# A fused transformer block on Trainium2: tokens loaded first, a convolution ahead of level exponents, and the expert loop's scatter after the up projection

## The chip, the core and the metric

One core of a Trainium2 chip runs the whole block as one program. The metric is the device time of that core in microseconds, the median over several executions. All data are float32. Five engines take part: TensorE (PE; its weight loads are PEld), VectorE (DVE), ScalarE (ACT), GpSimd (POOL) and the queue engine SyncE (SP), which here issues every DMA.

## What is computed

One layer over 256 latent and 256 context tokens of width 1024. The reference, cut to the parts that the change touches (`...` marks what is left out):

```python
hl = modulate(rmsnorm(xl, norm1_g[i]), mod_l[0], mod_l[1])      # h = x / rms * g * (1 + scale) + shift
hc = modulate(rmsnorm(xc, norm1_g[i]), mod_c[0], mod_c[1])
fl = mixer_inputs(hl, p, grid_rows)                             # h @ w_in, short convolutions, decays
...
(gla_c, gla_l), (rw_c, rw_l), (ssd_c, ssd_l) = token_mixers(fc, fl)
xl = xl + mod_l[2] * mixer_output(fl, gla_l, rw_l, ssd_l, p)
hl = modulate(rmsnorm(xl, norm2_g[i]), mod_l[3], mod_l[4])
xl = xl + mod_l[5] * moe(hl, p)                                 # then a final rmsnorm

def moe(h, p):                                                  # top 4 of 32 experts
    ...
    for e in range(N_EXPERTS):
        gu = t @ p['moe_w_gu'][e] + p['moe_b_gu'][e]
        glu, lin = jnp.split(gu, 2, axis=-1)
        ...
        act = glu * jax.nn.sigmoid(SWIGLU_ALPHA * glu) * (lin + 1.0)
        y = y + gates[:, e:e + 1] * (act @ p['moe_w_down'][e] + p['moe_b_down'][e])
```

## The kernel before, in words

Every engine has a program of its own, written out in order; semaphores tie them together. PSUM is handled by a table of rounds (`Rounds`, `round_table`): each named product ("B", "l3", "xs0", "roots") has a group of banks, PE *claims* it (waits until the product before it in that group is drained), *fills* it, and DVE or ACT *drain* it. Groups 0 to 3 are pairs of banks, group 4 is one bank. Three stages are touched.

**The opening** (up to the first projection). SP issues the small parameters, the identity matrix, then for each of eight blocks k of 128 features a piece of the modulation weights (`load_ada(k)`, 1 MB) and one called `opened` (block k of the transposed tokens, beside the first projection weights for it). The four `tokens` transfers (512 KB each, tokens by rows) come behind block 0's two. ACT squares and sums the token rows (line 880), takes the root (883), DVE the reciprocal (1320), and PE spreads the 512 reciprocals over all partitions (`roots_spread`, PSUM "roots"). PE also computes the modulation: `modulation_row(k)` needs block k's two transfers, ACT copies the row (875), `modulation_columns(k)` turns it, DVE adds the bias (1309, 1317). DVE multiplies the raw transposed tokens by the spread reciprocals (1322 for k = 0, 1307 later), ACT and DVE write the modulated hidden state hT (889, 1325), and PE multiplies it by the weights of block k and goes on to the modulation of block k + 1. To fill its waits PE runs `stay_busy(n)`, n products of the identity (line 1986), with n from `WARM`. Each float32 matmul stands in the trace as two records.

**The levels.** The gated linear attention is computed over eight nested block sizes. For level i + 1 POOL forms exponent arguments (lines 788 to 791) in one of two buffers, ACT exponentiates (`level_exp(i)`, line 945), DVE multiplies them with the keys (`level_keys(i)`, line 1424), PE multiplies in two parts (`level(i+1, 0)` and `level(i+1, 1)`, rounds "l0" to "l8" of group 2), and DVE writes the scores out with a mask (`level_out(i)`: 1249, 1251 and 1254), which drains that round. Beside them PE computes the projections B, C, xs0, xs1, z0 and z1. B and xs0 share PSUM group 0, so xs0 can start only when DVE has drained B. B's convolution is begun by ACT (`conv_start`, 899), done by DVE in 12 instructions that read PSUM (`convolve`, 1345) and ended by ACT (906). DVE also folds incoming modulation weights into sums (`multiplied(n)`, 1290 and 1292).

**The expert loop.** All 32 experts are computed, each for 64 slots of tokens. Expert n needs six weight blocks of 2048 KB (four of w_gu, two of w_down). They are brought by SP into a ring of eight slots; `load_slot` (668) waits until PE has freed the slot. Three further slots take weights of expert 20 ahead of the loop. PE's order in `expert` is: `up`, eight steps k over the hidden dimension, two steps a ring slot. After step 0 it calls `between`, which is `scatter_before`: the matmuls that add the previous expert's output to the first half of the tokens (`scatter(…, (0,))`, two matmuls, one for each half of the columns), then two transposes that select the tokens of the next scatter (`select_back`, 2860). After up comes the second half's scatter, then `turn` (2869) of the first activated half, the gather of a later expert's tokens, `turn` of the second half, and `down`. DVE reads up's result for the activation (1864 to 1871) and, after down, writes the expert's weighted output `ye` (1893). The matmuls here go through a helper at line 1972, those of scatter being the 64-row ones. The last expert uses `up_by_halves`, which finishes one half of the columns early.

Of the kernel before, what the change touches and what calls it, by code (L numbers as in the profile page):

```python
# [169 lines left out]
WARM = (10, 4, 26, 7)  # L170
# [21 lines left out]
def round_table():  # L192
    t = []
    for m in range(KD):
        t += [(f"row{m}", 4, 1), (f"col{m}", 2, 1 if m == KD - 1 else 0)]
        if m == 0:
            t.append(("roots", 2, 0))
# [77 lines left out]
def hybrid_block(nc, a):  # L275

    with ExitStack() as ctx:
# [202 lines left out]
        ident_in = sem("ident_in")  # L480
# [10 lines left out]
        silu_c, root_ready, rms_ready, mod_ready = named("silu_c root_ready rms_ready mod_ready")  # L491
# [18 lines left out]
        f_sq, out_ready, out_done, half_up, bias_up = named("f_sq out_ready out_done half_up bias_up")  # L510
# [76 lines left out]
        for s, width, kind, n in loads:  # L587
            base[s] += 1
# [41 lines left out]
        def _(sp):  # L630
# [11 lines left out]
            sp.dma_start(Cb(C_ID), a["consts"][:, 0:P]).then_inc(ident_in, 16)  # L642
            for k in range(KD):
                if k == 1:
                    for i in range(4):
                        sp.dma_start(xtok[:, i, :], a["tokens"][i]).then_inc(x_in[i], 16)
                load_ada(k)
                sp.dma_start(opened[:, k, :], a["opened"][k]).then_inc(slot_full[ADA_SLOTS[k]], 16)
                if k in (3, 6):
                    load_ada(8 + k // 4)  # L650
# [204 lines left out]
        def _(act):  # L855
# [16 lines left out]
            def row_copied(m):  # L872

                R.arrived(act, f"row{m}")
                R.drained(f"row{m}", act.copy(modrow[:, 64 * m:64 * m + 64], pair(f"row{m}", 512)[:, 64 * m:64 * m + 64]))

            row_copied(0)
# [6 lines left out]

            for k in range(KD):
                act.wait_ge(mod_ready, k + 1)
                if k == 0:
                    act.wait_ge(rms_ready, 2)
# [63 lines left out]

            level_exp(0)
            level_exp(1)
            conv_start("B")
# [302 lines left out]
        def _(dve):  # L1258
# [18 lines left out]

            def multiplied(n):
# [24 lines left out]
            for k in range(KD):  # L1303
                s, nth = place["opened", k]
                dve.wait_ge(slot_full[s], 16 * nth)
                if k:
                    step(dve.tensor_tensor(raw[:, k, :], raw[:, k, :], pair("roots")[:, 0:NT], ALU.mult))
# [10 lines left out]
                if k == 0:  # L1318
                    dve.wait_ge(root_ready, 1)
                    dve.reciprocal(small[:, 12:16], small[:, 8:12]).then_inc(rms_ready, 1)  # L1320
                    R.arrived(dve, "roots")
# [646 lines left out]
        def _(pe):  # L1968
# [919 lines left out]
            def expert(m, i, gathers, opening=None, aside=None, past=False):  # L2888
# [25 lines left out]
                if not first:  # L2914
                    scatter((i + 1) % 2, (1,))
# [163 lines left out]
```

## Time and profile before

| | us |
|---|---|
| median of 3 runs (1314.92, 1322.54, 1323.43) | 1322.54 |
| the profiled execution, its whole device time | 1317.88 |
| its span, first to last instruction | 1316.1 |

The span of the profiled execution is 1.8 us below its device time; what is taken from the trace is compared with 1317.88, which is 4.7 below the median. PE is busy for 1246.7 us of the span (95%), DVE for 401.6, ACT for 261.2, POOL for 50.4. The DMA engines move 456.13 MB. The granted TensorE clock is 0.996 of full speed on average. Times below are microseconds from the start of the span; a number in square brackets behind an instruction is how long its engine stood idle before it and what ended that.

### The profile page before, as it was taken

What the parts mean: (1) busy time and instruction counts of PE and PEld (TensorE: products, weight loads), DVE (VectorE), ACT (ScalarE), POOL (GpSimd) and SP (SyncE); (2) the same over time, 40 slices, a digit from 0 to 9 for tenths busy, and PEclk for the clock granted to TensorE, in tenths of its full rate; (3) what the DMA queues carried; (4) which work ended last, traced back from release to release, by engine and by line L of the source; (5) the groups of instructions that cost most, each with busy time, mean ns of one, the idle gap of its engine ahead of it and who ended that gap; (6) DMA issues with size and microseconds to landing.
All of it is one profiled execution on the core that took longest, in us unless ns stands there. A gap on an engine that the chain in (4) does not pass through costs nothing.

```text
span 1316.1 us, 22353 instructions
## 1 busy us (share of the span) xinstructions
PE 1246.7 (95%) x9546; PEld 589.9 (45%) x9546; DVE 401.6 (31%) x906; ACT 261.2 (20%) x601; POOL 50.4 (4%) x89
## 2 busy tenths in 40 slices
PE   8999999889899999999999999999999999999997
PEld 6464656678874333333333333333333333333333
DVE  1457766654442211121111221211221111121112
ACT  3142218543332110111100110100111010011001
POOL 0022100311100000000000000000000000000000
PEclk9999999999999999999999999999999999999999
DMA  9953520243479999999999999999999999999994
GB/s 377 397 193 128 220 108 1 90 144 96 125 279 384 425 426 427 428 429 429 426 429 429 430 427 427 429 430 429 427 428 427 428 428 427 428 427 428 426 427 200
DMA packets 41407, 456.13 MB, mean 347 GB/s; under 512 B 4624, under 2 KB 4880, under 8 KB 12912
## 3 DMA queue, kind: packets, MB, share of 16 engines
q1 hardware_dynamic: 41328, 454.96, 83.1%
q8 instruction: 64, 1.05, 0.3%
q14 instruction: 15, 0.12, 0.0%
HBM read 453.89 MB, written 1.05 MB: 346 GB/s over the span
## 4 chain that ended last, share of the span: by engine, by line
PE 84%; DVE 6%; DMA 5%; issue 2%; ACT 1%; POOL 0%; SPq 0%; DVEq 0%
PE PS L1972 80%; DMA arena<-in_moe_w_gu 3%; DMA arena<-in_moe_b_down 2%; PE PS L2869 2%; DVE arena L1865 1%; DVE arena L1868 1%; DVE arena L1871 1%; PE PS L2860 1%; DVE arena L1345 1%; PE PS L1986 1%; DVE arena L1864 1%; DMA arena<-in_opened 1%; PE PS L2464 0%; POOL arena L790 0%; DVE arena L1965 0%
## 5 line engine op out<-in xcount | busy, mean ns | idle before, releaser
L1972 PE MATMUL PS<-arena 128*64 128x512 f32 (+12 forms) x9174 | 1200.3, 402 | 26.0 <-issue 10.4
L1972 PEld LDWEIGHTS PS<-arena 64*64 64x64 f32 (+6 forms) x9174 | 549.4, 144 | 627.4 <-issue 563.6
L1864 DVE TENSOR_SCALAR arena<-PS 128x256 f32<-128x256 f32 x64 | 38.6, 604 | 505.8 <-PE PS L1972 505.8
L1178 ACT ACTIVATE arena<-arena 128x256 f32<-128x256 f32 x64 | 26.7, 417 | 477.2 <-DVE arena L1864 477.2
L1893 DVE TENSOR_TENSOR arena<-PS,arena 128x512 f32<-128x512 f32 x32 | 22.1, 692 | 214.5 <-PE PS L1972 214.5
L1188 ACT COPY arena<-PS 128x256 f32<-128x256 f32 x32 | 11.9, 373 | 281.0 <-PE PS L2860 281.0
L2869 PE MATMUL PS<-arena 128*128 128x128 f32 x128 | 26.3, 287 | 32.6 <-DVE arena L1871 32.6
L1169 ACT ACTIVATE arena<-PS,arena 128x128 f32<-128x128 f32 x128 | 48.2, 457 | 35.7 <-PE PS L1972 35.7
L2869 PEld LDWEIGHTS PS<-arena 128*128 128x128 f32 x128 | 14.3, 141 | 59.9 <-DVE arena L1871 43.0
L1630 DVE COPY arena<-PS 128x384 f32<-128x384 f32 (+2 forms) x48 | 23.4, 490 | 54.1 <-PE PS L1972 53.7
L1865 DVE TENSOR_SCALAR arena<-PS 128x256 f32<-128x256 f32 x64 | 39.1, 612 | 0.0
L1345 DVE SCALAR_TENSOR_TENSOR arena<-PS,arena 128x255 f32<-128x255 f32 (+5 forms) x68 | 32.6, 481 | 20.2 <-ACT arena L980 14.0
L1292 DVE SCALAR_TENSOR_TENSOR arena<-arena 128x2048 f32<-128x2048 f32 x14 | 33.1, 2363 | 7.0 <-DMA arena<-in_ada 6.9
L1091 ACT COPY arena<-PS 128x384 f32<-128x384 f32 (+2 forms) x48 | 20.5, 427 | 58.7 <-PE PS L1972 58.6
L1868 DVE SCALAR_TENSOR_TENSOR arena<-arena 128x256 f32<-128x256 f32 x64 | 27.2, 425 | 3.9
L1871 DVE TENSOR_TENSOR arena<-arena 128x256 f32<-128x256 f32 x64 | 27.2, 426 | 2.3
L1183 ACT COPY arena<-PS 128x256 f32<-128x256 f32 x64 | 23.7, 370 | 4.3 <-PE PS L2869 4.3
L1840 DVE TENSOR_SCALAR arena<-arena 128x128 f32<-128x128 f32 x64 | 19.1, 342 | 0.0
L1986 PE MATMUL PS<-arena 128*128 128x128 f32 x94 | 14.5, 323 | 3.3 <-DMA arena<-in_consts 3.3
L2860 PEld LDWEIGHTS PS<-arena 128*128 128x128 f32 x64 | 6.5, 141 | 24.3 <-issue 24.3
L1827 DVE TENSOR_SCALAR arena<-arena 128x64 f32<-128x64 f32 x64 | 15.7, 308 | 2.0 <-PE PS L1972 1.9
L1986 PEld LDWEIGHTS PS<-arena 128*128 128x128 f32 x94 | 13.7, 233 | 3.5 <-DMA arena<-in_consts 3.3
(263 smaller groups left out, 395.0 us busy)
## 6 DMA issues: line engine op xcount, KB each, us to landing
arena<-in_moe_w_gu SPq DMA_DIRECT2D x124, 2048.0 KB, 22.5
arena<-in_moe_w_down SPq DMA_DIRECT2D x63, 2048.0 KB, 24.3
arena<-in_ada SPq DMA_DIRECT2D x24, 1024.0 KB, 7.4
arena<-in_w_in SPq DMA_DIRECT2D x4, 2048.0 KB, 9.6
arena<-in_moe_w_gu SPq DMA_DIRECT2D x32, 256.0 KB, 3.0
arena<-in_opened SPq DMA_DIRECT2D x8, 576.0 KB, 19.0
arena<-in_tokens SPq DMA_DIRECT2D x4, 512.0 KB, 8.5
arena<-in_w_out SPq DMA_DIRECT2D x2, 1024.0 KB, 5.8
```

The source lines that it names most:

```text
L1169: ins = act.activation(hg[:, buffer, k, :], PS[:, bank, P * j:P * j + P], ACT.Identity, bias=scales[:, 1, k:k + 1], scale=scales[:, 0, k:k ...
L1178: act.activation(sgm[:, 256 * half:256 * half + 256], glu[:, 256 * half:256 * half + 256], ACT.Sigmoid, scale=ALPHA).then_inc(sig_ready, 1)
L1183: act.copy(actT[:, 2 * half:2 * half + 2].rearrange("p a b c -> p (a b c)"), src).then_inc(actT_ready, 1)
L1292: ins = dve.scalar_tensor_tensor(out=flat, in0=slots[sl], scalar=by_row, in1=flat, op0=ALU.mult, op1=ALU.add)
L1345: ins = dve.scalar_tensor_tensor(out=d_, in0=s_, scalar=wgt, in1=d_, op0=ALU.mult, op1=ALU.add)
L1864: dve.tensor_scalar(by_rest(glu), of_half(0), LIMIT, None, ALU.min).then_inc(glu_ready, 1)
L1865: dve.tensor_scalar(by_rest(lin), of_half(1), LIMIT, -LIMIT, ALU.min, ALU.max).then_inc(moe_vec, 1)
L1868: dve.scalar_tensor_tensor(out=lin[:, cols], in0=lin[:, cols], scalar=1.0, in1=glu[:, cols], op0=ALU.add, op1=ALU.mult).then_inc(moe_vec, 1)
L1871: dve.tensor_tensor(act_[:, cols], lin[:, cols], sgm[:, cols], ALU.mult).then_inc(act_ready, 1)
L1972: ins = pe.matmul(out, lhsT, rhs, start=start, stop=stop, skip_group_check=skip)
L1986: pe.matmul(PS[:, 0, 0:P], ident, ident, start=True, stop=True)
L2869: ins = pe.transpose(dst[:, c * P:c * P + P], act_[:, (2 * half + c) * P:(2 * half + c + 1) * P], ident)
```

## The change

1. **Opening.** The four token transfers are issued ahead of block 0's. Block 0's `opened` gets a semaphore of its own. "roots" becomes the first round of its group, and `roots_spread` goes ahead of `modulation_row(0)`. The reciprocal is the first thing DVE does after its constants, and block 0 is scaled like the others. ACT squares the tokens ahead of copying row 0. The filler products go from 10 + 4 + 26 + 7 to 30 + 3 + 6.
2. **Levels.** On ACT `conv_start("B")` goes ahead of `level_exp(0)`. On DVE `convolve(0, "B")` goes ahead of `level_keys(0)`, and `level_keys(1)` behind `level_out(0)`. On PE xs0 no longer has level 1's first part ahead of it; every part of levels 1 to 4 stands one project step later.
3. **Expert loop.** The scatter for the first half of the tokens moves from inside up to the place of the other half's scatter behind up. Only the selection stays inside.

```diff
-WARM = (10, 4, 26, 7)
+WARM = (30, 3, 6)
...
+            for i in range(4):
+                sp.dma_start(xtok[:, i, :], a["tokens"][i]).then_inc(x_in[i], 16)
             for k in range(KD):
-                if k == 1:
-                    for i in range(4):
-                        sp.dma_start(xtok[:, i, :], a["tokens"][i]).then_inc(x_in[i], 16)
                 load_ada(k)
...
+            conv_start("B")
             level_exp(0)
             level_exp(1)
-            conv_start("B")
             level_exp(2)
...
+            dve.wait_ge(root_ready, 1)
+            dve.reciprocal(small[:, 12:16], small[:, 8:12]).then_inc(inverse_ready, 1)
...
+            convolve(0, "B")
             level_keys(0)
+            level_out(dve, 0)
             level_keys(1)
-            level_out(dve, 0)
-            convolve(0, "B")
             multiplied(14)
...
+            roots_spread()
             modulation_row(0)
             stay_busy(WARM[1])
             modulation_columns(0)
             stay_busy(WARM[2])
-            roots_spread()
-            stay_busy(WARM[3])
...
+            project_in("xs0", 0, early)
             level(1, 0)
-            project_in("xs0", 0, early)
+            project_in("xs0", 0, late)
             level(1, 1)
...
             project_in("xs1", 1, late)
             sums_by_feature(1)
+            level(4, 1)
...
                     if not first:
                         pe.wait_ge(ye_ready, n + 1)
                         pe.wait_ge(sw_ready, n + 1)
-                        scatter((i + 1) % 2, (0,))
                     select_back(n)
...
                 if not first:
-                    scatter((i + 1) % 2, (1,))
+                    scatter((i + 1) % 2, (0, 1))
                 turn(n, 0, PS[:, 3, 0:256])
```

On PE the opening reads, up to the second block's projections, before (L1986 is the filler, 32x64 the modulation row, 64x4 its columns, 128x128 x4 at L1972 the spread of the roots, 128x256 the first projection):

```order
L1986 MATMUL PS<-arena 128x128 x10
L1972 MATMUL PS<-arena 32x64 x32
L1986 MATMUL PS<-arena 128x128 x4
L1972 MATMUL PS<-arena 64x4 x2
L1986 MATMUL PS<-arena 128x128 x26
L1972 MATMUL PS<-arena 128x128 x4
L1986 MATMUL PS<-arena 128x128 x7
L1972 MATMUL PS<-arena 128x256
```

and in the changed kernel (L1982 is the filler, L1968 the rest):

```order
L1982 MATMUL PS<-arena 128x128 x30
L1968 MATMUL PS<-arena 128x128 x4
L1968 MATMUL PS<-arena 32x64 x32
L1982 MATMUL PS<-arena 128x128 x3
L1968 MATMUL PS<-arena 64x4 x2
L1982 MATMUL PS<-arena 128x128 x6
L1968 MATMUL PS<-arena 128x256
```

The spread has moved ahead of the row, and the filler that stood ahead of it (26) is gone; 30 products now stand at the start.

At the end of the moved levels PE has, before, from the second part of level 4 on (128x128 x4 is one level part, 128x512 x4 half a tile of xs1, L2040 the turning of the modulation sums, 128x256 x8 a tile of z0, L2333 B by token):

```order
L1972 MATMUL PS<-arena 128x128 x4
L1972 MATMUL PS<-arena 128x512 x4
L2040 MATMUL PS<-arena 128x128 x4
L1972 MATMUL PS<-arena 128x128 x4
L1972 MATMUL PS<-arena 128x256 x8
L2333 MATMUL PS<-arena 128x128 x4
```

and in the changed kernel:

```order
L1968 MATMUL PS<-arena 128x128 x4
L1968 MATMUL PS<-arena 128x512 x4
L2036 MATMUL PS<-arena 128x128 x4
L1968 MATMUL PS<-arena 128x128 x8
L1968 MATMUL PS<-arena 128x256 x8
L2328 MATMUL PS<-arena 128x128 x4
```

There the second part of level 4 and the first of level 5 have become one block of eight, with nothing between them (the first row is now the first part of level 4).

In the expert loop PE's row, before, from an expert's scatter inside up on (128x512 is a scatter matmul, L2860 the selection, 64x512 up and down, L2869 a turn, 128x128 x8 the gather; the register rows are left out of what moved):

```order
L1972 MATMUL PS<-arena 128x512 x2
L2858 ISA
L2860 MATMUL PS<-arena 128x128 x2
L1972 MATMUL PS<-arena 64x512 x32
L1972 MATMUL PS<-arena 128x512 x2
L2865 REGISTER_ALU
L2869 MATMUL PS<-arena 128x128 x2
```

and in the changed kernel:

```order
L2853 ISA
L2855 MATMUL PS<-arena 128x128 x2
L1968 MATMUL PS<-arena 64x512 x32
L1968 MATMUL PS<-arena 128x512 x4
L2860 REGISTER_ALU
L2864 MATMUL PS<-arena 128x128 x2
```


## Rows read from the trace of the kernel before

**Rows 1.** A stretch of the expert loop: stretch, length, busy time by engine, PEclk, DMA share, GB/s
```profile
500.00:600.00 100.00, 95.85 (x480) 35.19 (x478) 22.07 (x56) 12.59 (x35) 0.00 (x0) 1.00 1.01 428
```

**Rows 2.** The chain that ended last: start, length, what
```profile
939.91 34.06 DMA arena<-in_moe_w_gu
...
1212.87 9.79 PE PS L1972 x44
...
1240.96 9.79 PE PS L1972 x44
```

**Rows 3.** Timeline of expert 29's end and expert 30's start
```profile
1236.29 0.30 PEld L1972 LDWEIGHTS PS<-arena 64*128 64x128 f32 x4 [0.81 <-issue]
...
1238.51 0.44 PE L2869 MATMUL PS<-arena 128*128 128x128 f32 x2 [1.09 <-DVE arena L1871]
...
1249.62 0.30 PEld L1972 LDWEIGHTS PS<-arena 64*128 64x128 f32 x4 [0.81 <-issue]
1250.68 0.20 PEld L2860 LDWEIGHTS PS<-arena 128*128 128x128 f32 x2 [0.76 <-issue]
```

**Rows 4.** The third last and the last weight transfer: issue, and time until landed
```profile
L668 SPq DMA_DIRECT2D arena<-in_moe_w_gu x1: 332/332/332, 1256.6 to 1256.6; - x1
...
DMA to landing us min/median/max: 32.6/32.6/32.6
...
L668 SPq DMA_DIRECT2D arena<-in_moe_w_down x1: 333/333/333, 1264.6 to 1264.6; - x1
...
DMA to landing us min/median/max: 34.4/34.4/34.4
```

**Rows 5.** Timeline of the last expert: last quarter of up, first turn, down
```profile
1292.32 3.37 PEld L1972 LDWEIGHTS PS<-arena 128*64 128x64 f32 x32 [0.41 <-issue]
...
1297.15 0.44 PE L2869 MATMUL PS<-arena 128*128 128x128 f32 x2
...
1298.14 1.94 PE L1972 MATMUL PS<-arena 128*64 128x512 f32 x8 [0.55 <-ACT arena L1183]
...
1300.91 5.37 PE L1972 MATMUL PS<-arena 128*64 128x512 f32 x24 [0.46 <-ACT arena L1183]
```

**Rows 6.** The opening: the four token transfers with their landing times
```profile
L646 SPq DMA_DIRECT2D arena<-in_tokens x4: 432/477/823, 2.6 to 4.4; - x4
...
DMA to landing us min/median/max: 7.5/8.5/9.5
```

**Rows 7.** The opening's timeline: fillers, row 0, root, spread to first projection
```profile
3.33 4.64 PE L1986 MATMUL PS<-arena 128*128 128x128 f32 x20 [3.33 <-DMA arena<-in_consts]
...
8.98 1.94 PE L1972 MATMUL PS<-arena 128*32 128x64 f32 x64 [1.02 <-DMA arena<-in_opened]
...
13.09 6.07 PE L1986 MATMUL PS<-arena 128*128 128x128 f32 x52
...
15.38 0.30 ACT L883 ACTIVATE arena<-arena 128x4 f32<-128x4 f32 x1
...
21.53 18.66 PE L1972 MATMUL PS<-arena 128*128 128x256 f32 x270
```

**Rows 8.** Timeline of the levels: B's convolution, xs0's start, level_out(4), xs1's convolution, level_out(5), z0's end
```profile
97.26 1.43 ACT L899 ACTIVATE arena<-PS,arena 128x512 f32<-128x512 f32 x2
...
99.20 6.16 DVE L1345 SCALAR_TENSOR_TENSOR arena<-PS,arena 128x254 f32<-128x254 f32 x12
...
105.50 36.08 PE L1972 MATMUL PS<-arena 128*128 128x512 f32 x128 [2.81 <-DVE arena L1345]
...
138.00 1.35 DVE L1254 COPY_PREDICATED arena<-arena,PS 128x512 f32<-128x512 int32 x2 [3.42 <-PE PS L1972]
...
143.16 6.17 DVE L1345 SCALAR_TENSOR_TENSOR arena<-PS,arena 128x254 f32<-128x254 f32 x12 [0.89 <-DVE arena L1298]
...
149.24 1.36 DVE L1254 COPY_PREDICATED arena<-arena,PS 128x512 f32<-128x512 int32 x2
...
151.08 0.60 ACT L950 ACTIVATE arena<-PS 128x512 f32<-128x512 f32 x1 [0.66 <-PE PS L1972]
```

More of the change, by code:

```diff
@@ L871, in _ @@
             act.activation(small[:, 60:61], small[:, 59:60], ACT.Sqrt)
[L872 to L877, printed above, removed]
             for i in range(4):
@@ L883, in _, with row_copied @@
             act.activation(small[:, 8:12], small[:, 0:4], ACT.Sqrt, scale=1.0 / D, bias=small[:, 59:60]).then_inc(root_ready, 1)
+            def row_copied(m):
+                R.arrived(act, f"row{m}")
+                R.drained(f"row{m}", act.copy(modrow[:, 64 * m:64 * m + 64], pair(f"row{m}", 512)[:, 64 * m:64 * m + 64]))
+            row_copied(0)
             for k in range(KD):
                 act.wait_ge(mod_ready, k + 1)
-                if k == 0:
-                    act.wait_ge(rms_ready, 2)
                 act.activation(hT[:, k, L:NT], raw[:, k, L:NT], ACT.Identity, bias=mod[:, k, 0:1], scale=A1[:, k, 0:1]).then_inc(h_by_act, 1)
@@ L2019, in roots_spread @@
                 R.claim(pe, "roots")
[L2020 removed]
+                pe.wait_ge(inverse_ready, 1)
                 for t in range(4):
@@ L2181, in _ @@
             project_in("C", 1)
+            project_in("xs0", 0, early)
             level(1, 0)
-            project_in("xs0", 0, early)
+            project_in("xs0", 0, late)
             level(1, 1)
-            project_in("xs0", 0, late)
+            project_in("xs0", 1, early)
             level(2, 0)
-            project_in("xs0", 1, early)
+            project_in("xs0", 1, late)
             level(2, 1)
-            project_in("xs0", 1, late)
+            project_in("xs1", 0, early)
             level(3, 0)
-            project_in("xs1", 0, early)
-            level(3, 1)
             project_in("xs1", 0, late)
             modulation_sums(1)
+            level(3, 1)
+            project_in("xs1", 1, early)
             level(4, 0)
-            project_in("xs1", 1, early)
-            level(4, 1)
             project_in("xs1", 1, late)
             sums_by_feature(1)
+            level(4, 1)
             def running_sums(q):
@@ L2910, in expert @@
                     return
-                up(n, at, tokens_of, scatter_before, first)
+                up(n, at, tokens_of, select_before, first)
                 if opening:
@@ L2914, in expert @@
                 if not first:
-                    scatter((i + 1) % 2, (1,))
+                    scatter((i + 1) % 2, (0, 1))
                 turn(n, 0, PS[:, 3, 0:256])
```

43 lines of the change are left out of this document (19 added, 24 removed).

## The prediction

> **What bounds the kernel now.** I read the DMA share by stretches first, then the chain that ended last, the landings of the last transfers, and the timeline of the stages that the change touches. In the expert loop the DMA engines are busy without a gap, at 428 GB/s [rows 1]. That is the number to start from. One weight block is 2048 KB, 2.097 MB, so it takes 4.9 us, and the third last and the last land at 1256.6 + 32.6 = 1289.2 and 1264.6 + 34.4 = 1299.0, twice 4.9 us apart, the one between at 1294.1 [rows 4]. An expert has six: 29.4 us of transfers. PE needs 1240.96 - 1212.87 = 28.1 us for one [rows 2]. So PE, at 96% busy, looks like the bound, and is in fact the faster of the two: it lives on the lead that the weights got before the loop, losing 1.3 us of it an expert. Around expert 20 the lead is gone, and the chain goes through a weight transfer for 34 us [rows 2]. Expert 20's three extra blocks (14.7 us of transfer) then restore a lead, on which the remaining experts live. At the end PE starts the last quarter of up at 1292.3 with weights that landed at 1289.2: a lead of 3.1 us. The first block of down is used at 1298.1 (landed 1294.1), the second at about 1300.91 + 8/24 of 5.37 = 1302.7 (landed 1299.0): 4.0 and 3.7 us [rows 4, 5]. Those 3 to 4 us are all that a faster PE can win in the loop. Ahead of the loop DMA is lightly used and the time is set by PE with DVE, ACT and POOL between.
>
> **The expert loop.** Removed inside up: two scatter matmuls, from 1249.62 to the selection at 1250.68, 1.06 us on the weight-load row; by the streaming rate, four records of 512 columns run in two pairs, 0.86 us [rows 3]. Added behind up: the same 0.86 us. There it lies beside the activation. Up's last load is followed by the scatter at 1236.29, and the first turn starts at 1238.51 after PE has stood idle 1.09 us for DVE [rows 3]. 1.09 - 0.86 leaves 0.2 us, so behind up it is hidden. PE's expert becomes 28.1 - 0.9 = 27.2 us, and 31 experts would save 27 us, if PE bound. It doesn't: 29.4 us of transfers stay 29.4. The lead is used up sooner (2.2 us an expert instead of 1.3), PE waits for weights from about expert 12 on, and again before the end: from expert 21 on it gains 10 times 0.9 = 9 us on a lead that was 3.1 at the last up. Freed slots come earlier, but they only join a queue that already holds some 30 us of work [rows 4]. What is left is the catch-up at the end: the last quarter of up moves from 1292.3 to 1289.2, -3.1. In the last expert the added scatter is not hidden. There half the columns finish early, DVE is ready sooner, and the first turn follows the one scatter at 1297.15 with no idle time of its own [rows 5]; two scatters put it 0.85 us later. Down then starts at 1298.1 - 3.1 + 0.85 = 1295.9 and its second half at 1300.5, both behind their landings, so nothing else bites. Sum: **-3.1 + 0.85 = -2.2 us**. Ends: -3.1 if the extra scatter hides there too; +0.85 where the transfers already set the end before the change (no lead to catch up).
>
> A rule bears on the size of the cut. The rows show 1.06 us for 0.86 us of streaming, 0.2 more, when PE goes from the 128x64 tiles of up to the 64x128 tiles of the scatter [rows 3]. The Trainium skill (TensorEngine Tiling (Array Packing), Key Properties) says that changing the tiling mode drains TensorE; the trace agrees, and by it the move saves a switch too, making the cut 1.06 instead of 0.86. With PE as the bound that would be 33 instead of 27 us; with the transfers as the bound it changes nothing.
>
> **The opening.** Before, the tokens land up to 4.4 + 9.5 = 13.9 [rows 6], but the first projection starts only at 21.53 [rows 7]. ACT has the root at 15.38 + 0.30, and then PE is still inside its 26 filler products, 13.09 to 19.16; the spread, the scaling by DVE and ACT's hT (2.4 us together) come behind. So it is the filler that holds the start, 3.3 us behind the reciprocal. Now the same bytes come in another order. Block 0's two transfers take the place in the queue that the last token transfer had, so I take 13.9 for their landing instead of 8.98 less a little, and the tokens come about 3.9 us earlier, by 10.0. ACT has its last squares at 11.2 and DVE the reciprocal at 12. PE's 30 products are 60 records. The first 20 of before took 4.64 us (0.232 each, the rate of the 1.2 GHz level) and those from 13.09 on 0.117 each (2.4 GHz) [rows 7]. There the rate rose about 4 us after PE resumed at 8.98; the first 4.64 us had not raised it. Without the break I take 28 slow records: 3.33 + 6.5 + 32 x 0.117 = 13.6. Ends: 20 slow, 12.6; all slow, 17.2. Then the spread (8 records, 0.9) to 14.5, row 0 (1.94 slow, half that fast: 1.4) to 15.9, its copy with three fillers and the columns 1.0 to 16.9, DVE 0.6, hT to PE 0.65: the first projection at 18.1, 3.4 us earlier. At best (block 0's landing at 13.9 binds) 17.2, -4.3. Each later block takes PE longer than its transfers take, and all transfers behind block 0 come after the same bytes as before, so the gain is kept: **-3.4 us** (-4.3 to +2.5, the latter all slow, below).
>
> The number of slow matmuls at a start is not fixed, says the Trainium skill (TensorE: Matmul & The Clock Gate, The HAM clock gate): it varies between runs of one kernel. No run here shows that; it is a reason to keep the slow end of this term in the range.
>
> **The levels.** Before, xs0 waits 2.81 us, until DVE has drained B at 105.36 [rows 8]. DVE starts that convolution at 99.20, behind two level_keys and a level_out, and ACT's start of it (97.26) stands behind two exponents. PE arrives at 105.50 - 2.81 less level 1's first part (0.6), 102.0. B is full C's 32 records (0.214 each, 256 columns at the high clock) and a level part before that, at about 94.3. Now ACT starts then and takes 1.43, DVE starts at 95.7, and B is drained at 95.7 + 6.16 = 101.9. The wait of 2.81 us goes. What is late next? The block from 105.50 to 142.0 (36.5 us) gets level 1's first part (0.6) and starts at 102.0: it ends at 139.1 instead of 142.0, now with level 4's second part as its last piece. But level 5's first part follows directly and needs level 4 drained: level_out(4), 1.3 us (1.35 in [rows 8]). PE waits, to 140.5. And DVE, in order, does level_out(4), keys(5), a sum of weights, then xs1's convolution, then level_out(5). Before, level_out(4) started at 138.00 because level 4 was complete early, and level_out(5) ran at 149.24 to 150.6 [rows 8], just in time for level 6, for which PE was ready at 151.1 (z0 ends there [rows 8]). Now the chain starts at 139.1: 4.3 us to the convolution (143.16 - 138.00 less 0.89 of waiting [rows 8]), 6.1 for it, 1.35: level 5 drained at 150.9. PE, ready earlier, waits for it and starts level 6 at 150.9 to 151.1. POOL's third set of exponent arguments now starts only after keys(0) at 102.6, some 6 us later, and with it C's convolution; its slack covers that (drained at about 111; PE needs C's banks for xs1, four half tiles of 3.4 us and four level parts after 102, at 118). Sum: **0 us**. Ends: -2.8, the whole wait, if xs1's convolution is ready sooner than I make it; +1 if POOL or DVE come later.
>
> **Sum.** -3.4 + 0 - 2.2 = -5.6 us: 1317.9 becomes 1312.3 for an execution like the profiled one. That one lies 4.7 below the median of the three; the four known times have a mean of 1319.7, and 5.6 below that is 1314; the median lies above the mean, so I say 1315.
>
> **The rivals.**
> - *The loop's cut arrives in full* (PE bounds): -27 - 3.4 = -30, 1289 us. For it: PE 96% busy and the chain almost all PE. Against it: the DMA share of 1.01 and 29.4 against 28.1 us. It would need transfers at over 460 GB/s (12.58 MB in 27.2 us), which no stretch shows.
> - *The transfers already set the end in ordinary executions*: the known times reach 1323, 5.5 above the profiled one, and a rate lower by 0.5% would cost 4.5 us over the loop and take the lead of 3.1 away. Then the loop gives +0.85 and the opening -3.4: -2.5, 1317 from the mean.
> - *The levels' wait goes for good*: -3.4 - 2.8 - 2.2 = -8.4, 1311. Against it: the DVE chain above.
> - *Slower: the opening runs at the low clock.* The 30 products end at 17.2, spread 1.9, row 1.94, its copy and columns with slow fillers 1.7, DVE and ACT 1.25: first projection at 24.0, +2.5; with +0.85 at the last scatter and no lead to catch up, +3.3, 1323. It decides from where the fillers end later than about 15.5. For it: 4.64 us of work at the start of before did not raise the clock. Against it: unbroken work did, in 4 us, from 8.98 on.
>
> **How the numbers follow.** Forecast 0.62, transfers already the bound 0.15, levels in full 0.08, slower 0.07, loop in full 0.08 (a misjudged DMA bound). About 1% (13 us) is what a measurement of this kernel can tell from no change. Only the full cut passes that, and perhaps a median that falls badly: faster 0.11, same 0.85, slower 0.04. The range takes the forecast's ends (-9 to +1 about 1319.7) and the spread of single executions: 1307 to 1322.
>
> **What would show it.** Opening: the first projection at 17.2 to 18.6, records of 0.117 us before 13.6. Levels: no idle time before xs0 near 98.5 (102 less the opening), a new one of about 1.4 us before level 5 and one before level 6. Loop: PE's expert at 27.2 us in the first ten and 29.4 from about the twelfth, new waits for w_gu inside up, DMA share still 1.0, the last block landing some 3.4 us earlier, and the last first turn 0.85 us later behind up. I am wrong if experts stay at 27.2 us to the end, or if the last landing moves by more than the opening and levels do.

## The result, and the profile of the changed kernel

The changed kernel takes 1310.09 us (median of 11 runs, 1308.87 to 1313.48); the kernel before, 11 runs, 1318.09 us. The ratio is 0.9941, 95% interval 0.9926 to 0.9956: 7.8 us faster, between 5.8 and 9.8. The forecast was 1315 and 5.6 us faster. Of the 4.9 us between 1315 and 1310, 2.5 come from the starting point: 5.6 below the 1318.09 now measured would be 1312.5. The two profiled executions are 1311.81 (span 1309.9) and 1317.88 us: -6.1.

**The opening**, its timeline (start, duration, engine, line, operation, tiles, count, idle time before and what ended it), the answer to [rows 6, 7]:

```profile
3.14 9.10 PE L1982 MATMUL PS<-arena 128*128 128x128 f32 x60 [3.14 <-DMA arena<-in_consts]
10.66 0.30 ACT L874 ACTIVATE arena<-arena 128x4 f32<-128x4 f32 x1
12.07 2.09 PE L1968 MATMUL PS<-arena 128*128 128x128 f32 x72
13.39 0.69 DVE L1309 TENSOR_TENSOR arena<-arena,PS 128x512 f32<-128x512 f32 x1 [2.23 <-DMA arena<-in_opened]
16.61 54.35 PE L1968 MATMUL PS<-arena 128*128 128x256 f32 x620
```

The fillers end at 12.2, block 0 lands just ahead of 13.4, spread and row 0 run at the high clock (72 records in 2.09 us) and the first projection starts at 16.61 instead of 21.53, 4.9 us earlier. The reciprocal is there at 11.2, so the fillers still hold the start, by 0.9 us: in all six profiles with 30 fillers the spread begins when they end (12.07 to 13.50) and the first projection follows 4.54 us behind.

**The levels**, timeline, the answer to [rows 8]:

```profile
90.85 6.17 DVE L1341 SCALAR_TENSOR_TENSOR arena<-PS,arena 128x254 f32<-128x254 f32 x12 [2.10 <-ACT arena L894]
...
132.88 1.35 DVE L1249 COPY_PREDICATED arena<-arena,PS 128x512 f32<-128x512 int32 x2 [5.87 <-PE PS L1968]
...
134.38 4.36 PE L1968 MATMUL PS<-arena 32*128 32x128 f32 x24 [1.54 <-DVE arena L1249]
...
137.19 6.17 DVE L1341 SCALAR_TENSOR_TENSOR arena<-PS,arena 128x254 f32<-128x254 f32 x12
...
143.28 1.35 DVE L1249 COPY_PREDICATED arena<-arena,PS 128x512 f32<-128x512 int32 x2
...
144.78 15.51 PE L1968 MATMUL PS<-arena 32*128 32x128 f32 x80 [1.30 <-DVE arena L1249]
```

The wait before xs0 is gone. PE waits 1.54 us for level_out(4) ahead of level 5 and 1.30 us for level_out(5) ahead of level 6, as the prediction had it. Level_out(5) starts 5.96 us earlier than before (143.28, 149.24 [rows 8]), 4.92 of them from the opening.

**The loop.** Stretches of it, in the columns of [rows 1], then three pieces of the chain that ended last, then waits of PE (in total, times, longest): for weights in the changed kernel, and for the activation ahead of an expert's first turn, changed and before:

```profile
500.00:600.00 100.00, 99.43 (x499) 35.95 (x499) 18.73 (x49) 11.84 (x33) 0.00 (x0) 1.00 1.01 428
900.00:1000.00 100.00, 93.87 (x466) 33.13 (x462) 17.25 (x43) 10.07 (x28) 0.00 (x0) 1.00 1.01 428
```

```profile
447.00 8.74 PE PS L1968 x40
...
473.97 8.73 PE PS L1968 x40
...
704.53 34.61 DMA arena<-in_moe_w_gu
```

```profile
PE PS L1968 <- DMA arena<-in_moe_w_gu: 25.5, 37, 1.9
PE PS L2864 <- DVE arena L1867: 7.9, 31, 1.5
PE PS L2869 <- DVE arena L1871: 32.6, 31, 1.5
```

The DMA share is 1.01 at 428 GB/s early and late, while PE's share falls from 99% to 94%. An expert of PE takes 473.97 - 447.00 = 27.0 us at first; from 704.5 us on, about the twelfth expert, the chain goes through the weights. Before, PE waited for these 1.2 us in all. The wait ahead of the turn has shrunk from 32.6 to 7.9 us over 31 waits, 0.8 us each: behind up the added scatter is hidden, as the prediction had it.

**The end.** Issue and landing of the last block of up and of the last block, the answer to [rows 4], and the last expert's timeline, that to [rows 5]:

```profile
L665 SPq DMA_DIRECT2D arena<-in_moe_w_gu x1: 333/333/333, 1250.3 to 1250.3; - x1
...
DMA to landing us min/median/max: 35.3/35.3/35.3
...
L665 SPq DMA_DIRECT2D arena<-in_moe_w_down x1: 333/333/333, 1260.1 to 1260.1; - x1
```

```profile
1285.63 3.37 PEld L1968 LDWEIGHTS PS<-arena 128*64 128x64 f32 x32 [0.49 <-DMA arena<-in_moe_w_gu]
...
1291.32 0.44 PE L2864 MATMUL PS<-arena 128*128 128x128 f32 x2
...
1292.32 1.94 PE L1968 MATMUL PS<-arena 128*64 128x512 f32 x8 [0.55 <-ACT arena L1178]
```

Both transfers take 35.3 us: they land at 1285.6 and 1295.4, 3.6 us earlier than before. The last quarter of up starts on its landing (1285.63) instead of 3.1 us behind it (1292.32 against 1289.2 [rows 4, 5]); the first turn follows after 5.69 us instead of 4.83 [rows 5].

**Given back.** Level_out(5) is 6 us early, the last landing 3.6. The missing 2.4 us are lost between 340 and 365 us, where the change has touched nothing. The same place in both kernels, first the changed one, then the one before:

```profile
353.19 1.64 PE L1968 MATMUL PS<-arena 64*64 64x64 f32 x54 [1.71 <-issue]
...
355.57 3.85 PE L1968 MATMUL PS<-arena 64*64 64x128 f32 x48 [0.75 <-DVE arena L1626]
```

```profile
357.98 1.02 PE L1972 MATMUL PS<-arena 64*64 64x64 f32 x46 [1.15 <-issue]
...
360.60 2.33 PE L1972 MATMUL PS<-arena 64*64 64x128 f32 x48 [0.75 <-DVE arena L1630]
```

The same 48 records take 3.85 us in one and 2.33 in the other, since the granted clock stands at 0.5, the 1.2 GHz level, from 356 to 359 us; the pauses before it ("issue": nothing that the profile shows) are longer too.

### The profile page after: what moved, and what is told of

It is laid out like the page before. It is cut to its first block, busy times and chain, and to the rows that moved or that the text cites. A ratio compares the mean times of both kernels' runs of the same rounds, so it can differ in the third digit from the quotient of the medians.

```text
span 1309.9 us, 22318 instructions
## 1 busy us (share of the span) xinstructions
PE 1242.3 (95%) x9530; PEld 590.0 (45%) x9530; DVE 402.6 (31%) x906; ACT 261.3 (20%) x601; POOL 52.6 (4%) x89
## 3 DMA queue, kind: packets, MB, share of 16 engines
q8 instruction: 64, 1.05, 0.3%
HBM read 453.89 MB, written 1.05 MB: 347 GB/s over the span
## 4 chain that ended last, share of the span: by engine, by line
PE 65%; DMA 26%; DVE 6%; issue 2%; ACT 1%; SPq 0%; DVEq 0%
PE PS L1968 61%; DMA arena<-in_moe_w_gu 24%; DMA arena<-in_moe_b_down 2%; DVE arena L1341 1%; PE PS L2864 1%; DVE arena L1861 1%; PE PS L1982 1%; DVE arena L1867 1%; DVE arena L1864 1%; PE PS L2855 1%; DVE arena L1860 0%; PE PS L2459 0%; DVE arena L1290 0%; ACT arena L894 0%; DVE arena L1249 0%
## 5 line engine op out<-in xcount | busy, mean ns | idle before, releaser
L1968 PE MATMUL PS<-arena 128*64 128x512 f32 (+11 forms) x9174 | 1197.3, 402 | 49.5 <-DMA arena<-in_moe_w_gu 25.5
L1968 PEld LDWEIGHTS PS<-arena 64*64 64x64 f32 (+5 forms) x9174 | 551.0, 145 | 645.2 <-issue 523.3
L1341 DVE SCALAR_TENSOR_TENSOR arena<-PS,arena 128x255 f32<-128x255 f32 (+5 forms) x68 | 32.6, 481 | 18.3 <-ACT arena L975 14.0
L2864 PE MATMUL PS<-arena 128*128 128x128 f32 x128 | 26.4, 288 | 7.9 <-DVE arena L1867 7.9
L2864 PEld LDWEIGHTS PS<-arena 128*128 128x128 f32 x128 | 14.2, 141 | 35.3 <-DVE arena L1867 24.4
L2855 PEld LDWEIGHTS PS<-arena 128*128 128x128 f32 x64 | 6.5, 141 | 25.6 <-issue 25.6
L785 POOL TENSOR_TENSOR arena<-arena 128x128 f32<-128x128 f32 x8 | 10.8, 1350 | 112.9 <-ACT arena L933 84.6
L1982 PE MATMUL PS<-arena 128*128 128x128 f32 x78 | 11.6, 318 | 3.1 <-DMA arena<-in_consts 3.1
```

The lines of the kernel that those rows point to most:

```text
L1341: ins = dve.scalar_tensor_tensor(out=d_, in0=s_, scalar=wgt, in1=d_, op0=ALU.mult, op1=ALU.add)
L1968: ins = pe.matmul(out, lhsT, rhs, start=start, stop=stop, skip_group_check=skip)
L1982: pe.matmul(PS[:, 0, 0:P], ident, ident, start=True, stop=True)
L2864: ins = pe.transpose(dst[:, c * P:c * P + P], act_[:, (2 * half + c) * P:(2 * half + c + 1) * P], ident)
```

## The experiments

All ratios are to the kernel before, with 95% intervals.

**e1_open_only.** The kernel before with this of the diff and what hangs on it:

```diff
-WARM = (10, 4, 26, 7)
+WARM = (30, 3, 6)
+            for i in range(4):
+                sp.dma_start(xtok[:, i, :], a["tokens"][i]).then_inc(x_in[i], 16)
             for k in range(KD):
```

> The kernel before with the opening part alone (the levels and the expert loop stand as before; the two semaphores of the last expert are one, as in the changed kernel). The profile of the changed kernel shows the first projection 4.9 us earlier (16.61 against 21.53), and its level 6 6.3 us earlier, but behind 370 us only 3.4 us are left: the granted clock fell to 0.5 there for 4 us, and two stops of PE were 1.0 us longer together. Theory A: those 2.6 us belong to that one execution. Then this kernel has its first projection at 16.6 and ends 4.9 us earlier than before: ratio 0.9963, 1313.2 us. Theory B: whatever brings the front forward is given back around 355 us: -2.3 us, ratio 0.998. Theory C, the prediction's size: -3.4 us, ratio 0.9974, first projection at 18.1.

Measured: 0.9956 (0.9939 to 0.9972), 5.8 us, between 3.7 and 8.0. First projection at 16.61. Theory A's 0.9963 lies in the interval. B's 0.998 and C's 0.9974 lie outside, C's by a hair, and C's first projection at 18.1 did not come in this profile either.

**e2_levels_only.** The kernel before with the three edits of the levels (ACT's `conv_start("B")` first, DVE's `convolve(0, "B")` first, the new interleaving on PE).

> The kernel before with B's convolution ahead of the level exponents and the levels' new order on PE, nothing else. Theory A, from the profile of the changed kernel (the wait of 2.81 us before xs0 gone, new ones of 1.5 before level 5 and 1.3 before level 6 in its place, level 6 1.3 us earlier than the opening alone explains): level 6 starts at 149.8 instead of 151.1, -1.3 us, ratio 0.999. Rival, the prediction's term: 0 us, level 6 at 151.1, ratio 1.000. Rival: the wait goes for good, -2.8 us, level 6 at 148.3, ratio 0.998.

Measured: 0.9993 (0.9978 to 1.0007). Such an effect is too small for the times; its profile began 2.3 us earlier in the opening (below), so levels are compared relative to the first projection, from there to the start of level_out(6): before 134.5 us (156.03 - 21.53), here 133.6, e1 133.2 (149.83 - 16.61), the changed kernel 133.2. So e1, with the old order and its wait, is as quick as the changed kernel: where the clock does not fall, the new order is worth nothing. What the kernel before has and e1 has not is this, right behind the wait for xs0, first before, then e1:

```profile
104.00:106.00 2.00, 0.50 (x1) 0.50 (x2) 1.93 (x4) 1.54 (x2) 0.00 (x0) 0.78 0.00 0
106.00:108.00 2.00, 2.00 (x3) 0.67 (x2) 2.00 (x2) 0.45 (x1) 0.00 (x0) 0.50 0.00 0
```

```profile
100.00:102.00 2.00, 1.20 (x3) 0.68 (x4) 1.96 (x3) 1.26 (x2) 0.00 (x0) 1.00 0.00 0
102.00:104.00 2.00, 2.00 (x6) 0.76 (x4) 1.97 (x4) 0.00 (x0) 0.00 (x0) 1.00 0.22 29
```

The number behind POOL's count, PEclk, is 0.78 and 0.50 in the one and 1.00 in the other: a fall of the clock behind the wait, in one execution and not in the other. The block of 128 records behind it took 36.08 us [rows 8] and 34.59 in e1.

**e3_scatter_only.** The kernel before with the scatter moved:

```diff
-                        scatter((i + 1) % 2, (0,))
                     select_back(n)
...
-                    scatter((i + 1) % 2, (1,))
+                    scatter((i + 1) % 2, (0, 1))
```

> The kernel before with the scatter moved behind up, nothing else. Theory: the weight transfers bind. PE's expert is 27.05 us until about the twelfth, then 29.4 on average, with waits for weights; the last block of weights lands when it did before; the last quarter of up starts on its landing instead of 3.1 us behind it, and the first turn stands 0.86 us later behind it: -2.2 us, ratio 0.9983, 1315.9 us. Rival, PE binds: -31 us, ratio 0.976. Rival, the transfers already set the end in ordinary executions: +0.85 us, ratio 1.0006.

Measured: 0.9982 (0.9963 to 1.0), 2.4 us, with an interval that reaches from 4.9 to nothing. The transfers bind, and PE's rival of 31 us is out. The last quarter of up starts 1.1 us behind its landing (1293.3), not on it, and the turn 5.69 us behind:

```profile
1294.43 3.37 PEld L1972 LDWEIGHTS PS<-arena 128*64 128x64 f32 x32 [0.41 <-issue]
...
1300.12 0.44 PE L2869 MATMUL PS<-arena 128*128 128x128 f32 x2
```

Here the clock had fallen from 1272 to 1276 us, behind the 1.52 us that PE waits between the turns of the last but one expert. The kernel before has that fall too (1268 to 1274), so part of the 3.1 us by which it started its last quarter behind the landing was owed to it; the changed kernel's profile has none.

**e4_last_inside.** The changed kernel, the last expert's scatter of the first half back behind its first quarter:

```diff
-                    up_by_halves(n, at, tokens_of, select_before)
-                    scatter((i + 1) % 2, (0, 1))
+                    up_by_halves(n, at, tokens_of, half_before)
+                    scatter((i + 1) % 2, (1,))
```

> The changed kernel, but in its last expert the first token half's scatter stands inside up again, behind its first quarter. Theory: PE consumes a quarter of up in 4.85 us and a block lands every 4.9, so what is put in behind the first quarter is not absorbed: the last quarter starts 0.5 to 0.7 us later instead of on its landing, and the first turn follows it after 4.8 instead of 5.7 us. Net -0.15 to -0.35 us, ratio to before 0.9939 to 0.994. Rival, the wait for weights hides it wholly: last quarter still on its landing, -0.86 us, ratio 0.9934.

Measured: 0.9949 (0.9929 to 0.9968), no difference that can be told from the changed kernel. Its profile has the fall at 1264 to 1270, so it is held against e3, which has one too: the quarter starts 2.2 us behind its landing against 1.1, and the turn 4.83 us behind the quarter against 5.69. Nothing of the 1.1 us is absorbed, and the last sum of DVE stands 6.4 us behind the last landing against 6.2: net +0.2, where the theory had -0.15 to -0.35. (The whole end is 15.8 against 16.0, but that difference arises behind the last sum, 9.4 against 9.8.) Inside up or behind it, the last expert's extra scatter costs nearly the same.

**e5_before_light and e6_after_light.** Both kernels with lighter transfers. A reloaded slot gets three quarters of its columns and keeps old values in the rest, so these two kernels do not compute the layer; they serve for the time alone:

```diff
-            def load_slot(r, e, s):
+            def load_slot(r, e, s, width=4096):
...
-                load_slot(r, q // PER, q % PER)
+                load_slot(r, q // PER, q % PER, 3072)
...
-                            load_slot(r, m * GROUP + i, s)
+                            load_slot(r, m * GROUP + i, s, 3072)
```

> The kernel before, in which from the first reloaded slot of the ring on each weight block's transfer brings the first three quarters of its columns only (the rest of a slot keeps what it held; PE's work is unchanged). An expert's transfers then take 22 us instead of 29.4, PE's work 28.1. Theory, transfers bind but PE of the kernel before lives on its lead: its waits for weights, 1.2 us in all, go, and that is all: ratio 0.999. Rival: the transfers slow PE or its experts themselves (a shared memory, a queue); then the experts become shorter than 28.1 us and the ratio is under 0.99.

> The changed kernel with the same lighter transfers. Theory: its 25.5 us of waits for weights, in 37 waits, are where the cut of PE's work went, and they go: PE's expert is 27.05 us to the end, ratio to before 0.975, 1284.6 us, 32 us ahead of the kernel before with the same transfers. Rival: the cut is not there for another reason (another engine, ye or the counters come later): 1310 us, ratio 0.994, as the changed kernel.

Measured: 0.9981 (0.9963 to 0.9998) and 0.9702 (0.9688 to 0.9716), medians 1315.7 and 1278.0 us. The same 100 us of the light kernels, before and changed:

```profile
500.00:600.00 100.00, 95.86 (x482) 35.08 (x482) 21.34 (x55) 12.59 (x35) 0.00 (x0) 1.00 0.86 340
```

```profile
500.00:600.00 100.00, 99.43 (x496) 35.41 (x494) 16.88 (x41) 10.44 (x30) 0.00 (x0) 1.00 0.90 349
```

This is the experiment that settles the loop. With DMA off the bound, the kernel before gains almost nothing and the changed one 32 us. Between their medians lie 37.7 us. In the profiles 32.2 of the difference lie behind the first products of 128x32 (1320.8 - 396.98 = 923.8 against 1277.2 - 385.62 = 891.6), where the loop is; the rest lies ahead of it, and e5's profiled execution is 6.9 us above its median. My expected 32 us was too little; I had left out the opening. It also tells the size of the cut. An expert of PE takes 28.05 us in e5 (484.47 to 764.94 for ten) and 27.00 in e6 (471.82 to 741.81 for ten): 1.05 us, as on the weight-load row (1.06), not the 0.86 of pure streaming. The Trainium skill (TensorEngine Tiling (Array Packing), Key Properties) says that changing the tiling mode drains the engine; the 0.2 us of difference per expert agree, though no run here separates the change of mode from other causes.

**e7_filled_wait.** The kernel before, with

```diff
             level(1, 0)
+            for _ in range(11):
+                pe.matmul(PS[:, 7, 0:P], ident, ident, start=True, stop=True)
             project_in("xs0", 0, early)
```

> The kernel before, with 11 filler products on PE (22 records of 0.117 us, 2.6 us, into a bank that nobody uses then) in the wait of 2.81 us ahead of xs0, nothing else. In the profile of before the granted clock is 0.5 from 105 to 109 us, right behind that wait; with only the opening changed (e1) the same wait of 2.83 us was followed by no fall, and levels 1 to 6 then took 1.3 us less. Theory: the fall is a consequence of the wait. Then there is none here, and the third last drain of a level before 165 us starts 133.2 us behind the first projection, as in e1 and the changed kernel, against 134.5 in before: -1.4 us where before has the fall, ratio 0.999 to 1. Rival: the fall comes from elsewhere; then it stands at the same place in spite of the fillers in some executions, and nothing is gained.

Measured: 0.9972 (0.996 to 0.9983), 3.7 us, more than expected. PE's timeline, the fillers and xs0's block:

```profile
100.38 2.72 PE L2184 MATMUL PS<-arena 128*128 128x128 f32 x22
103.36 34.59 PE L1972 MATMUL PS<-arena 128*128 128x512 f32 x128 [0.26 <-DVE arena L1345]
```

The wait has become 0.26 us, the block has its short length, and the clock does not fall there. What the other 2 us are is not settled; that profile has no fall near 250 and 350 us either, and its pauses of PE that wait for nothing the profile shows, between 150 and 398 us, add up to 8.3 us, against 10.4 to 12.6 in before, e2, e3 and e5.

**e8_warm_turn.** The changed kernel, with

```diff
+                if not gathers:
+                    keep_warm(6)
                 if gathers:
```

> The changed kernel with six filler products (12 records of 0.117 us) between the two turns of the last but one expert, where PE otherwise waits 1.51 us for DVE since no gather stands there. In five of six profiles so far the granted clock falls to 0.5 right behind that wait, for some 4 us (1.7 us lost); in that of the changed kernel it did not. Theory: with the fillers it never falls there, the last quarter of up starts on its landing, and the end lies 14.5 us behind the last landing, as in the changed kernel's profile, instead of 16: up to -1.1 us against the changed kernel in ordinary executions, ratio to before 0.993. Rival: the fall has nothing to do with the wait: it is there again behind 1262 us, and the end lies 16 us behind the last landing.

Measured: 0.9941 (0.9928 to 0.9953), as the changed kernel. The mechanism is as the theory says, in PE's timeline of the last but one expert:

```profile
1262.66 1.50 PE L1968 MATMUL PS<-arena 128*128 128x128 f32 x12
1264.35 0.44 PE L2864 MATMUL PS<-arena 128*128 128x128 f32 x2 [0.18 <-DVE arena L1867]
1264.72 10.71 PE L1968 MATMUL PS<-arena 128*64 128x512 f32 x64
```

64 records in 10.71 us is the high clock (e3: 12.42 for 64 at the same place); the last quarter starts on its landing, the end lies 14.5 us behind the last landing. That gain of up to 1.1 us does not show in the median.

**e9_tuned.** Fillers 24, 1, 4 at the start, six more ahead of level 5, those of e8, and in the last expert:

```diff
-                    scatter((i + 1) % 2, (0, 1))
                     turn(n, 0, PS[:, 3, 0:256])
-                    down(n, at, lambda: turn(n, 1, PS[:, 0, 0:256]))
+                    scatter((i + 1) % 2, (0,))
+
+                    def second():
+
+                        turn(n, 1, PS[:, 0, 0:256])
+                        scatter((i + 1) % 2, (1,))
+
+                    down(n, at, second)
```

> The changed kernel with four edits, each for a wait that its profile shows. Opening: 24, 1 and 4 filler products instead of 30, 3 and 6, since the reciprocal is there at 11.17 and the fillers end at 12.07, and the row's copy at 14.43 and its fillers at 14.95: first projection 0.7 to 1.1 us earlier (the landing of block 0 at 13.4 allows 1.2). Level 5: six filler products in the wait of 1.54 us: no fall of the clock there. Last but one expert: six between the turns, as in e8. Last expert: the first turn ahead of the scatter, the scatter's halves behind the two turns: down starts 0.5 to 0.9 us earlier behind the last quarter of up (6.7 us in the changed kernel's profile). Theory: all four arrive, -1.5 to -3 us against the changed kernel, ratio to before 0.992. Rival: the opening's gain is lost to the clock (fewer records before row 0), and down waits for the copies as long as before: ratio 0.994 as the changed kernel.

Measured: 0.9913 (0.99 to 0.9927), 1306.55 us: 11.5 us faster than before, and its interval only just touches that of the changed kernel. Down starts 5.63 us behind the start of the last quarter of up instead of 6.69, and the end lies 14.0 us behind the last landing. The opening's 0.9 us are lost at once:

```profile
15.74 1.56 PE L1968 MATMUL PS<-arena 128*128 128x256 f32 x4
...
18.64 0.69 DVE L1309 TENSOR_TENSOR arena<-arena,PS 128x512 f32<-128x512 f32 x1 [3.13 <-DMA arena<-in_opened]
18.75 5.58 PE L1968 MATMUL PS<-arena 128*32 128x64 f32 x78 [1.45 <-DMA arena<-in_opened]
```

PE now waits 1.45 us for block 1 to land (0.48 in e12): with fewer fillers the opening is bound by its transfers.

**e10_short_fill.** The changed kernel with `WARM = (12, 3, 6)`.

> The changed kernel with 12 filler products at the start instead of 30, so that PE stands idle from about 8.9 until the reciprocal at 11.2. Rival from the prediction (the opening at the low clock): the spread takes 1.9 us and row 0 1.94, copy and columns 1.7, DVE and ACT 1.25, first projection at 18.0 or later, +1.4 us against the changed kernel's 16.6. Theory: it needs the unbroken work, so this is what happens, and the first projections run at the low clock too for some us. Other rival: the clock rises with the time and not with the work: first projection at 15.9 (block 0's landing and DVE decide), -0.7 us.

Measured: 0.9968 (0.995 to 0.9986), half of the changed kernel's gain; the two intervals overlap narrowly, at 0.9950 to 0.9956. The spread and row 0:

```profile
11.46 3.65 PE L1968 MATMUL PS<-arena 128*128 128x128 f32 x72 [2.95 <-DVE arena L1274]
...
17.60 54.35 PE L1968 MATMUL PS<-arena 128*128 128x256 f32 x620
```

72 records in 3.65 us instead of 2.09: behind an idle time of 2.95 us they run at the low clock. From the start of the spread to the first projection it takes 6.14 us instead of 4.54, but the spread starts earlier (11.46), so the first projection comes 1.0 us later than in the changed kernel's profile and inside the 16.6 to 18.0 of the six with 30 fillers. The products that compute nothing buy the high clock; that they pay on balance is not shown. The medians differ by 3.6 us, which no row explains. The first projections themselves are not slow here (54.35 us, as in the changed kernel), against the theory.

**e11_spread_last and e12_fewer_fillers.** Two of e9's edits, each alone in the changed kernel.

> The changed kernel with e9's edit of the last expert alone: the first turn ahead of the scatter, its halves behind the two turns. In e9 down started 5.63 us behind the last quarter of up instead of 6.69, and the last sum of DVE 14.35 us behind it instead of 14.87, since down's first block (landed 1288.1) and the copies then decide. Theory: -0.5 us against the changed kernel, nothing else, ratio to before 0.9937. Rival: this edit is what made e9 3 us faster; ratio 0.992.

> The changed kernel with e9's opening alone: 24, 1 and 4 fillers instead of 30, 3 and 6. In e9 the first projection started at 15.74, 0.9 us ahead of the changed kernel's 16.6, but then PE waited 1.45 us for block 1 (landed at 18.6), and level 6's drain came at 150.6 against 149.8 to 151.5 in executions of the changed opening. Theory: the opening is bound by the transfers of block 1, the gain is 0, ratio 0.994. Rival: the opening's gain holds and makes up e9's: -1 us or more, ratio 0.993 or less.

Measured: 0.9926 (0.9906 to 0.9947) and 0.993 (0.991 to 0.995). Both intervals hold the changed kernel's ratio and e9's: which edit makes e9 faster is not told apart. In e11's profile the end lies 14.0 us behind the last landing, against 14.5 in e12 and the changed kernel, so the last expert's part is 0.5 us.

## Why the prediction was right, point by point

**The bound: right.** The loop is bound by its transfers at 428 GB/s, and PE lived on a lead. e3 (2.4 us alone) and the pair e5 and e6 (32 us once DMA is lighter) show both halves of it. PE waits from about the twelfth expert, as forecast. The last landing moved by 3.6 us (forecast 3.4), all of it from ahead of the loop: from the first products behind b_down's landing to the last landing it is 901.2 us before (1299.0 - 397.77) and 901.4 after (1295.4 - 394.01). In the twelve profiles with full transfers it is 901.2 to 901.8, with either place of the scatter, and once 902.8 (e4).

**The loop's term, -3.1 + 0.85 = -2.2: right, with a reserve.** The pair of profiles gives -3.1 and +0.86. But the 3.1 held a fall of the clock (1268 to 1274) that most executions have, and it came back in full only because the changed kernel's profile has no such fall. The end behind the last landing is 17.1 to 17.5 us with the scatter inside up (before, e1, e2, e7), 14.5 in the changed kernel and e12, and 15.3 to 16.0 in e10, e4 and e3, which have the fall: -1.1 to -2.6.

**The opening's term, -3.4 (-4.3 to +2.5): right by the mean of the profiles, too small for the pair and for e1.** In the pair the first projection moved by 4.9 us, beyond the term's best end. The step "28 slow records" was too many: 60 records in 9.10 us are, at 0.232 and 0.117 each, (9.10 - 60 x 0.117) / 0.115 = 18 slow ones; in e1 13, in e4 22, in e8 23, so the count differs between executions. Block 0 landed by 13.4 instead of 13.9. From the spread to the first projection it took 4.54 us, as forecast (18.1 - 13.6). And "the first 4.64 us had not raised it" was read from one execution. First projections with the old opening: 21.53, 19.22, 21.26, 21.04, 19.29 (before, e2, e3, e5, e7), mean 20.5; in e2 row 0 ran at the high clock:

```profile
8.42 1.10 PE L1972 MATMUL PS<-arena 128*32 128x64 f32 x64 [0.70 <-DMA arena<-in_opened]
```

With the new one: 16.61, 16.61, 17.64, 16.99, 18.04, 17.14 (changed, e1, e4, e6, e8, e11), mean 17.2. That is -3.3. The time of e1, which changes the opening alone, says more, -5.8 (-8.0 to -3.7); what lies between the two is open.

**The levels' term, 0 (-2.8 to +1): the mechanism right, the size off.** The two new waits came at 1.54 and 1.30 us where 1.4 was expected, and DVE's chain sets level 6. The step that failed is "the block from 105.50 to 142.0 (36.5 us)": I carried it over as it stood, though it held a fall of the clock of 1.5 us which the wait of 2.81 us had brought. With the wait gone the fall is gone: three of four profiles with the wait have it, none of the ten without (nine with the new order, and e7). From the first projection to level_out(6): 134.5, 134.5 and 136.0 us in before, e3 and e5, with wait and fall; 133.2 in e1, with the wait and no fall; 133.1 in e7, with the wait filled; 133.2 to 133.8 in seven profiles with the new order (e9 and e12, where PE waited for block 1, aside). Where an execution has the fall, as three of four did, the term is -1.3 or more.

**The sum.** By these, -3.3 for the opening, -1.3 for the levels and -1.1 to -2.6 for the loop make -5.7 to -7.2; measured -7.8, from -5.8 to -9.8. The parts measured alone (e1, e2, e3) add up to -5.8 - 0.9 - 2.4 = -9.1, each known to some 2 us. The profiled pair, -6.2 of span, came there on another way: -4.9, -1.0 (levels, without a fall in the one and with one in the other), -2.2, +2.4 given back near 350 us, and -0.4 behind the last sum (1316.1 - 1306.33 against 1309.9 - 1300.50). The stretch that gave back is a matter of the execution: from level_out(6) to the first products of 128x32 (391.32 before, 387.93 changed) it takes between 232.8 us (e12) and 240.0 (e2), 235.3 in the kernel before and 238.1 in the changed one, with unexplained pauses of PE of 8.3 to 12.6 us in all and no, one or two falls of the clock (none before, two in the changed kernel's profile). The pauses follow a count: in both kernels four of them end stretches of 126 or 127 records, and from the end of one pause to the end of the next it is then 3.3 to 4.4 us (264.20, 267.88, 271.61 before; 349.29, 353.19 changed). That points to the loading of instructions, for which the page lists a queue of its own (64 packets, 1.05 MB before), but it is argued, not tested. So the forecast's nearness to the profiled pair is in part luck: an opening 1.5 us better and levels 1.0 better than forecast met 2.4 us that were lost elsewhere.

**The rivals.** The loop's cut in full (-30) is out. "Transfers already set the end" is out: the +0.85 (1.0006) lies just outside e3's interval, and the profiles with the old scatter in the loop end 17.1 to 17.5 us behind the last landing, those of the new one sooner. "The levels' wait goes for good" gave -8.4 and 1311, nearer to the measured -7.8 and 1310 than the forecast, and is out in its mechanism all the same: two new waits took its place, and what went for good was the clock's fall. Its number is right by accident. "Slower: the opening at the low clock" did not occur; with fillers that stop early (e10) the spread and row 0 ran at the low clock, 1.6 us longer.

**Open:** e1's 5.8 us against 3.3 by the first projections, e7's 3.7 us, of which some 1.5 are explained, and which of e9's edits brings its 3.7 us (0.9941 - 0.9913, of 1318) against the changed kernel.

## What to carry to other kernels

Before pricing a cut of compute, divide the bytes of a loop's turn by the rate at a DMA share of 1.0: where that is longer than the engine's turn, a busy share of 96% is not the bound, and only the engine's lag behind the last landing can be won. When a duration is carried over from a trace, look at the granted clock in it: a wait of one or two us may be followed by some us at half speed, and both go together. Filling such a wait with products that compute nothing may win as much as removing it (e7), or nothing that a median shows (e8); they must end before what the engine waits for is there, as those of both openings did not.

## What the runs showed of the hardware

- The clock fell behind waits of PE as short as 1.5 us, and not each time. Between the turns of the last but one expert (1.5 us of waiting) it fell in 9 of 12 profiles without fillers and in neither of 2 with them; behind xs0's 2.8 us in 3 of 4, not with fillers; ahead of level 5 (1.54 us) in 3 of 8, not with fillers (one profile at each of these two places). A fall makes PE's work behind it 1.5 to 3 us longer (the block behind xs0's wait 36.08 in before and 37.56 in e5 against 34.59 in e1; the 24 records behind level 5's wait 6.01 in e2 against 4.36; 64 records 12.42 in e3 against 10.71).
- The granted clock reads 1.00 over the first products (before 8 us) of every kernel, though their records take 0.232 us, twice the 0.117 of later ones. At a start the durations tell the clock, not that column.
- One core drew 428 GB/s from 500 to 1000 us and beyond, and lighter transfers did not make PE's products shorter: its busy time in the same 100 us is 95.86 us with them and 95.85 without [rows 1].
